# Attention's q, k, v projection turned: tokens on partitions and weights moving, with the attention's stages written in another order

## The chip, the cores and the metric

One core of a Trainium2 chip runs the whole program. The metric is device microseconds for one execution; each kernel's figure is the median of its runs.

## The reference, cut to what matters

A trunk of two layers over x of 512 tokens by 1024 features in float32. The first layer mixes by convolution and pooling, the second by attention; each is followed by a gated MLP of width 2816. The change is in the attention.

```
def rmsnorm(x, g):
    x32 = x.astype(jnp.float32)
    y = x32 * lax.rsqrt(jnp.mean(x32 * x32, axis=-1, keepdims=True) + EPS)
    return (y * g.astype(jnp.float32)).astype(x.dtype)

def dilated_attention(xn, w_qkv, g_q, g_k, w_o, rel_table):
    qkv = (xn @ w_qkv).reshape(B, S, 3, N_HEADS, HEAD_DIM).astype(jnp.float32)
    q = rmsnorm(qkv[:, :, 0], g_q)
    k = rmsnorm(qkv[:, :, 1], g_k)
    v = qkv[:, :, 2]
...
    return o.reshape(B, S, D).astype(xn.dtype) @ w_o
```

There are 16 heads of 64 features. xn is the RMS norm of x over its 1024 features; q and k are normalised again, for each token and head. What is left out above is softmax(q k / 8 + bias) v over three dilated windows, merged.

## The kernel before

Every matrix product is done as three products of fp32r parts: an operand is split into its rounded value (`xh`, `wh`, `bh`) and the rest (`xl`, `wl`, `bl`), and hi x hi + hi x lo + lo x hi is summed in PSUM. `product` (L1082) issues the three: the weight tile of 128 x 128 is stationary, 512 tokens move, so results have features on partitions. Weights arrive by DMA (queue of SP) in four slots `raw0` to `raw3`, one "unit" each; ScalarE rounds a unit into `wh` (`round_unit`, L461, recorded at L466) and GpSimd subtracts to get `wl` (`rest`, L429, at L431). A slot's unit may be rounded when TensorE has used the one before (`s_unit`), and a load waits for GpSimd (`s_lo`).

The attention runs over 8 pairs of heads. Each engine has its instructions written out by hand in a function `stage(p, ...)`; the order in it is the order on the engine, and semaphores join the engines. For a pair the weights are four units: q (1024 columns), k (1024), v in two halves (512 each). TensorE's stage (L1316) does this: q's, k's and v's projections in pieces (`qkv_part`); the column sums of the squares of q and k (L1360: fp32 matmuls with two columns moving, 16 records a pair) into `bank3`; the norm factors, widened by VectorE to 64 columns each, turned onto features by `spread_norm` (L1389, twice 4 transposes); v turned to tokens by `turn_v` (L1380, 4 transposes). Between these stand the heads of the pairs in front: `score_blocks` (L1283, L1284: 8 products of 512, 384, 128 and 256 columns), `transposes` of the probabilities (L1294, 10 of 128 columns), `outputs` (L1312, 8 products into `obank`).

For a head the chain is: scores on TensorE; `scores` on VectorE (L968: adds the bias, takes the maximum, four pieces); `exponentials` on ScalarE (L699); `probabilities` on VectorE (L974 and L976); `transposes` on TensorE; `round_pt` on ScalarE (L716, two pieces) and `rest_pt` on VectorE (L982, two pieces), after which the score bank `spt` is free for the next head (`s_ptl`) and `outputs` can run; then `round_output` on ScalarE (L681) and `rest_output` on VectorE (L1041, L1044), after which the bank `obank` is free for the next head's `outputs` (`s_ol`).

Once a pair, VectorE computes 16 columns of reciprocal roots with small operations (L1005, L746 to L753), widens them (`widen`, L1052), multiplies (`normalise`, L1058), and makes the rests of q, k and v (L1018, L1031, L997).

At the end of the attention the output projection `w_o` begins (`wo_part`): its parts stand between the last heads' steps.

## Time and profile before

| | us |
|---|---|
| median of 3 runs (1132.41 to 2936.12) | 1132.81 |
| profiled execution | 1132.44 |
| its span in the trace | 1130.6 |
| TensorE busy | 1124.8 |
| VectorE busy | 582.0 |
| ScalarE busy | 487.7 |
| GpSimd busy | 461.7 |
| attention, first projection to last output, about | 504 to 742 in the span |

The page lists each engine's busy time, then the span in 40 slices, then groups of instructions by source line. A timeline lists single instructions, with equal neighbours merged (xN) and, in brackets, how long the engine was idle before and what released it. TensorE's records overlap: a matmul's row lasts until its result has drained, so the time that one takes from the engine is the distance to the next start. PE is TensorE, PEld its weight loads, DVE is VectorE, ACT ScalarE, POOL GpSimd.

### The profile page before, as it was taken

The page shows a single profiled execution, that of the slowest core. Times are in us where ns is not written, and L with a number is a line of the kernel's source. Part 1 is how long each engine was busy: PE and PEld are TensorE (multiplying, and loading weights), DVE is VectorE, ACT ScalarE, POOL GpSimd, SP SyncE. Part 2 cuts the span into 40 slices and gives each one's busy share as a digit, 9 for nine tenths or more (in the row PEclk, how much of TensorE's full clock was granted, in tenths as well). Part 3 has the DMA queues.
Part 4 walks back from the last instruction along what each step waited for, and adds up shares of the span by engine and source line. Part 5 has one row for each costly group of instructions (what it writes and reads, how often), then busy time and mean ns, then how long its engine had stood idle before and what let it go on. Part 6 is the DMA issues. An engine that isn't in the chain of part 4 may idle for free.

```text
span 1130.6 us, 16046 instructions
## 1 busy us (share of the span) xinstructions
PE 1124.8 (99%) x5228; PEld 936.7 (83%) x5228; DVE 582.0 (51%) x1047; ACT 487.7 (43%) x750; POOL 461.7 (41%) x221
## 2 busy tenths in 40 slices
PE   9999999999999999999999999999999999999998
PEld 7788888888888888888888888878888888888887
DVE  6875754545445412225777777777844545450000
ACT  5333444444444432324666666644534444341220
POOL 4454534354443445443223332134544344434442
PEclk9999999999999999999999999999999999999999
DMA  8232322322322233332322223122332222223331
GB/s 267 83 106 93 112 77 95 107 93 93 110 78 92 63 108 98 102 109 70 92 75 74 74 88 100 64 75 93 112 111 90 96 95 90 95 63 104 100 100 76
DMA packets 38925, 108.11 MB, mean 96 GB/s; under 512 B 4272, under 2 KB 7344, under 8 KB 38896
## 3 DMA queue, kind: packets, MB, share of 16 engines
q1 hardware_dynamic: 36560, 103.49, 28.7%
q10 hardware_dynamic: 2336, 4.24, 1.3%
q8 instruction: 17, 0.28, 0.1%
q14 instruction: 12, 0.10, 0.0%
HBM read 105.57 MB, written 2.15 MB: 95 GB/s over the span
## 4 chain that ended last, share of the span: by engine, by line
issue 45%; PE 33%; POOL 20%; DMA 1%; POOLq 0%; SPq 0%; ACT 0%; DVE 0%; DVEq 0%
POOL wl L431 20%; PE bank L1087 7%; PE bank L1086 7%; PE bank L1085 7%; PE spt L1085 4%; PE spt L1086 4%; PE spt L1087 4%; DMA raw<-w_in 1%; SPq L361 0%; POOLq L430 0%; POOLq L436 0%; PE obank L1087 0%; PE obank L1086 0%; PE obank L1085 0%; SPq L368 0%
## 5 line engine op out<-in xcount | busy, mean ns | idle before, releaser
L431 POOL TENSOR_TENSOR wl<-raw,wh 128x1024 fp32r<-128x1024 f32 (+2 forms) x214 | 457.5, 2144 | 644.2 <-ACT wh L466 644.2
L1085 PE MATMUL bank<-xh,wh 128*128 128x512 f32 x992 | 390.5, 394 | 0.0
L1087 PE MATMUL bank<-xh,wl 128*128 128x512 f32 x992 | 386.6, 390 | 0.0
L1086 PE MATMUL bank<-xl,wh 128*128 128x512 f32 x992 | 386.2, 389 | 0.0
L466 ACT ACTIVATE wh<-raw 128x1024 fp32r<-128x1024 f32 (+2 forms) x214 | 201.3, 945 | 145.1 <-PE spt L1087 139.4
L1087 PEld LDWEIGHTS bank<-xh,wl 128*128 128x128 f32 x992 | 186.2, 188 | 39.2
L1086 PEld LDWEIGHTS bank<-xl,wh 128*128 128x128 f32 x992 | 186.4, 188 | 37.4
L1085 PEld LDWEIGHTS bank<-xh,wh 128*128 128x128 f32 x992 | 186.3, 188 | 37.2 <-issue 0.4
L908 DVE TENSOR_TENSOR work<-bank,rstd 128x512 f32<-128x512 f32 x88 | 60.6, 691 | 225.0 <-PE bank L1087 223.1
L1085 PE MATMUL spt<-bh,wh 128*128 128x512 f32 x440 | 171.5, 390 | 0.4 <-POOL wl L431 0.3
L1086 PE MATMUL spt<-bl,wh 128*128 128x512 f32 x440 | 171.2, 389 | 0.0
L1087 PE MATMUL spt<-bh,wl 128*128 128x512 f32 x440 | 171.2, 389 | 0.0
L915 DVE SCALAR_TENSOR_TENSOR work<-work,par 128x512 f32<-128x512 f32 x176 | 128.5, 786 | 2.4 <-ACT work L582 1.8
L880 DVE TENSOR_TENSOR x<-spt,x 128x512 f32 (+1 forms) x27 | 18.6, 690 | 207.9 <-PE spt L1087 207.9
L1085 PEld LDWEIGHTS spt<-bh,wh 128*128 128x128 f32 x440 | 82.6, 188 | 18.3 <-POOL wl L431 0.7
L582 ACT ACTIVATE work<-work,par 128x512 f32<-128x512 f32 x44 | 35.9, 816 | 143.0 <-DVE work L908 143.0
L1087 PEld LDWEIGHTS spt<-bh,wl 128*128 128x128 f32 x440 | 82.6, 188 | 17.1
L1086 PEld LDWEIGHTS spt<-bl,wh 128*128 128x128 f32 x440 | 82.6, 188 | 17.1
L578 ACT ACTIVATE work<-work,par 128x512 f32<-128x512 f32 x44 | 35.9, 817 | 55.9 <-DVE work L908 55.9
L588 ACT ACTIVATE work<-work 128x512 f32<-128x512 f32 x44 | 27.9, 634 | 55.4 <-DVE work L915 55.4
L487 ACT ACTIVATE xh<-x,par 128x512 fp32r<-128x512 f32 (+1 forms) x24 | 17.4, 723 | 53.5 <-DVE acc L772 53.3
L772 DVE TENSOR_TENSOR acc<-acc,sq 128x512 f32<-128x512 f32 x24 | 40.0, 1668 | 0.0
(155 smaller groups left out, 938.3 us busy)
## 6 DMA issues: line engine op xcount, KB each, us to landing
raw<-w_up SPq DMA_DIRECT2D x88, 512.0 KB, 3.2
raw<-w_down SPq DMA_DIRECT2D x32, 384.0 KB, 3.1
raw<-w_down SPq DMA_DIRECT2D x32, 320.0 KB, 2.9
raw<-w_qkv SPq DMA_DIRECT2D x16, 512.0 KB, 3.6
raw<-w_in SPq DMA_DIRECT2D x14, 512.0 KB, 4.2
raw<-w_out SPq DMA_DIRECT2D x8, 512.0 KB, 3.2
raw<-w_qkv SPq DMA_DIRECT2D x16, 256.0 KB, 2.8
work<-bias_rows ACTq DMA_DIRECT2D x16, 256.0 KB, 3.1
```

Of the source, the lines that this page charges most:

```text
L431: nc.gpsimd.tensor_tensor(wl[s][:, 0:n], raw[s][:, 0:n], plain(wh[s][:, 0:n]), ALU.subtract).then_inc(s_lo, 1)
L466: nc.scalar.activation(wh[s][:, 0:n], raw[s][:, 0:n], ACT.Copy).then_inc(s_hi, 1)
L578: nc.scalar.activation(ug, zg[j][:, 2:], ACT.Identity, bias=col(i * 16 + (c + 3)), scale=col(i * 16 + (c + 2))).then_inc(s_id, 1)
L582: nc.scalar.activation(uu[j], zu[j][:, 2:], ACT.Identity, bias=col(i * 16 + (c + 7)), scale=col(i * 16 + (c + 6))).then_inc(s_id, 1)
L588: nc.scalar.activation(sg, ug, ACT.Silu).then_inc(s_silu, 1)
L772: nc.vector.tensor_tensor(acc[:], acc[:], squares, ALU.add).then_inc(s_acc, 1)
L880: nc.vector.tensor_tensor(tile(x, n), block_bank, tile(x, n), ALU.add).then_inc(s_x, 1)
L908: nc.vector.tensor_tensor(buf[:, 2:], bank[2 * j + n][:], rstd[:], ALU.mult).then_inc(s_z, 1)
L915: nc.vector.scalar_tensor_tensor(u, z[:, tap:tap + SEQ], col(i * 16 + (c + 4 * n + tap)), u, ALU.mult, ALU.add).then_inc(done, 1)
L1085: mm(dst, wh[s][:, w], hi, start=first, stop=False)
L1086: mm(dst, wh[s][:, w], lo, start=False, stop=False)
L1087: return mm(dst, wl[s][:, w], hi, start=False, stop=last)
```

## The change

The projection is turned. The 128 tokens of a tile of `xh` or `xl` are now stationary, and the pair's weights of q, k and v move together as 3 x 128 columns, so a product has 384 columns and its result has tokens on partitions: `token_product`, L1337 to L1339. There are four token tiles, done two at a time (`tokens`, `tokens_end`). A pair's four units now hold two k each for q, k and v (`QKV` is 768 columns in every slot; a load moves three pieces of 256 columns).

With tokens on partitions, v needs no turn, and the norm is per partition: ScalarE's `evacuate` copies q and k (256 columns), squares them (256) and rounds v scaled by the layer's norm factor (128); VectorE sums the squares (`sums`, two reductions of 512), computes 16 factors (`norm_factors`, twelve small operations), multiplies in place (`normalise`, 512 columns for q and for k), and takes v's rest in four pieces (`rest_v`). TensorE then turns q and k into `bank2` and `bank3` (`turn`, 4 transposes each); ScalarE rounds each half from there (`round_q`, `round_k`, `copy_k`), VectorE takes the rests (`rest_q`, `rest_k`). The sums by matmul, `spread_norm`, `widen`, `turn_v` and one `norm_spread` are gone.

All four engines' stages are written in a new order; loops over pairs are written out.

```diff
-QKV = (SLOT, SLOT, SLOT // 2, SLOT // 2)
+QKV = (6 * P,) * RING
...
+            def evacuate(pair, t):
+
+                b = token_bank(pair, t)
+                token_done(act, pair, t)
+                if pair >= 2:
+                    act.wait_ge(s_qt, pair - 1)
+                    act.wait_ge(s_kt, pair - 1)
+                at = slice(t * 2 * P, (t + 1) * 2 * P)
+                nc.scalar.activation(qk[pair % 2][:, at], bank[b][:, 0:2 * P], ACT.Copy).then_inc(s_qc, 1)
...
+                nc.scalar.activation(qksq[:, at], bank[b][:, 0:2 * P], ACT.Square).then_inc(s_qs, 1)
...
+                nc.scalar.activation(v_heads(pair, t, lo=False), v_part(b), ACT.Copy,
+                                     scale=small[:, 3, t:t + 1]).then_inc(s_vh, 1)
...
+            def stage(p):
+
+                new, mid, old, end = p < PAIRS, 1 <= p <= PAIRS, p >= 2, p >= PAIRS - 1
+                if new:
+                    evacuate(p, 0)
+                    evacuate(p, 1)
+                if mid:
+                    copy_k(p - 1, 0)
+                if old:
+                    round_output(p - 2, 0)
+                if mid:
+                    round_q(p - 1, 0)
+                    round_k(p - 1, 0)
+                if old:
+                    round_pt(2 * (p - 2) + 1)
+                if mid:
+                    round_k(p - 1, 1)
+                if new:
+                    round_weights(p + 1, 0)
+                if p == PAIRS:
+                    keep_w_o()
+                if mid:
+                    round_q(p - 1, 1)
+                if mid and end:
+                    copy_k(p - 1, 1)
+                if new:
+                    round_weights(p + 1, 1)
+                if mid:
+                    exponentials(p - 1, 0)
+                if new:
+                    evacuate(p, 2)
+                    evacuate(p, 3)
+                if mid and not end:
+                    copy_k(p - 1, 1)
+                if old and end:
+                    round_output(p - 2, 1)
+                if new and not end:
+                    round_weights(p + 1, 2)
+                if mid:
+                    round_pt(2 * (p - 1))
+                if new and end:
+                    round_weights(p + 1, 2)
+                if new:
+                    round_weights(p + 1, 3)
+                if old and not end:
+                    round_output(p - 2, 1)
+                if mid:
+                    exponentials(p - 1, 1)
...
+            def stage(p):
+                old = p >= 2
+                if old:
+                    transposes(2 * (p - 2))
+                tokens(p, 0, 0, 3)
+                if old:
+                    score_blocks(p - 2, 1)
+                tokens(p, 0, 3, 6)
+                tokens_end(p, 0)
+                if old:
+                    outputs(p - 2, 0)
+                turn(p - 1, 0)
+                turn(p - 1, 1)
+                tokens(p, 1, 0, 1)
+                if old:
+                    transposes(2 * (p - 2) + 1)
+                tokens(p, 1, 1, 4)
+                score_blocks(p - 1, 0)
+                tokens(p, 1, 4, 6)
+                tokens_end(p, 1)
+                if old:
+                    outputs(p - 2, 1)
...
+            transposes(2 * end - 2)
+            pe.wait_ge(s_vl, TB * PAIRS)
             wo_part(0, 0, 5)
+            wo_part(1, 0, 2)
+            score_blocks(end - 1, 1)
+            turn(end, 0)
+            turn(end, 1)
+            wo_part(1, 2, 5)
+            outputs(end - 1, 0)
             transposes(2 * end - 1)
             wo_part(0, 5, 6)
...
+            wo_part(1, 5, 6)
+            score_blocks(end, 0)
+            outputs(end - 1, 1)
```

The first `stage` above is ScalarE's, the second TensorE's. VectorE's stage, for pair p's new tokens, runs: `rest_v` 0 and 1, `probabilities` of the older pair's second head, `sums`, `rest_q` and `rest_k` of the first half, `rest_pt`, `scores` of p - 1's first head, `rest_output`, `probabilities`, `rest_v` 2, `sums`, `rest_v` 3, `rest_q` and `rest_k` of the second half, `rest_pt`, `rest_output`, `scores` of its second head, `norm_factors`, `normalise`. In the stage of the last pair, `rest_q` and `rest_k` stand ahead of the second `sums`, and `norm_factors` ahead of `rest_pt`.

Three places in the order of the built programs. First TensorE in a full stage, before: the sums of squares stand between v's projection and a head's scores (`par` holds the identity and the columns of 1/64; `work` holds q and k squared).

```order
L1087 MATMUL bank<-xh,wl 128x512
L1354 REGISTER_ALU
L1360 MATMUL bank<-par,work 128x2 [waits s_vl,s_qs]
L1360 MATMUL bank<-par,work 128x2 x7
L1281 ISA [waits s_kh,s_ql]
L1283 MATMUL spt<-bh 128x512 [waits s_ptl]
```

After, in a full stage, the turns of q and k stand between a head's outputs and the next products.

```order
L1440 MATMUL obank<-bl 128x128
L1397 MATMUL bank<-par,work 128x128 [waits s_ql,s_qn]
L1397 MATMUL bank<-par,work 128x128 x3
L1397 MATMUL bank<-par,work 128x128 [waits s_kl,s_kn]
L1397 MATMUL bank<-par,work 128x128 x3
L1337 MATMUL bank<-wh,xh 128x384 [waits s_vl]
L1338 MATMUL bank<-wl,xh 128x384
L1339 MATMUL bank<-wh,xl 128x384
```

The sums are gone, the turns have come, and the products have 384 columns of weights moving.

Second, VectorE at the attention's end, before, from the rests of the transposed probabilities (`spt`) of pair 6's second head to the scores of pair 7's first (`work` is the score tile).

```order
L982 TENSOR_TENSOR bl<-spt,bh 128x512 [waits s_pth]
L982 TENSOR_TENSOR bl<-spt,bh 128x768 [waits s_pth]
L1041 TENSOR_TENSOR sq<-obank,bh 64x512 [waits s_ol,s_oh]
L1044 TENSOR_TENSOR bl<-obank,sq 64x512 [waits s_of]
L965 MEMSET gate 128x1 [waits s_s,s_ta]
L968 ISA work,nmax<-spt,work 128x512
```

The same place after.

```order
L1023 TENSOR_TENSOR bl<-spt,bh 128x768 [waits s_pth]
L1050 SCALAR_TENSOR_TENSOR bh<-bank,gqs,bh 64x512 [waits s_qh]
L1057 SCALAR_TENSOR_TENSOR bl<-bank,par,bh 64x512 [waits s_kd,s_kh]
L1005 MEMSET gate 128x1 [waits s_s,s_ta]
L1008 ISA work,nmax<-spt,work 128x512
L1008 ISA nmax 128x1
L1008 ISA work,nmax<-spt,work 128x384
L1008 ISA nmax 128x1
L1008 ISA work,nmax<-spt,work 128x128
L1008 ISA nmax 128x1
L1008 ISA work,nmax<-spt,work 128x256
L1008 ISA nmax 128x1
```

The rest of the output (`obank`), which stood ahead of the scores, now comes after them, and `rest_q` and `rest_k` stand ahead.

Third, TensorE at that place after: the end of pair 7's first scores, then the outputs of pair 6's second head.

```order
L1411 MATMUL spt<-bh 128x256
L1412 MATMUL spt<-bl,bh 128x256
L1440 MATMUL obank<-bh,bl 128x512 [waits s_ptl,s_ol]
L1440 MATMUL obank<-bl 128x512
L1440 MATMUL obank<-bh,bl 128x384 [waits s_ptl]
```

As before, nothing stands between the two; the wait `s_ol` is for VectorE's rest of the output of pair 6's first head.

## Rows read from the trace of the kernel before

**Rows 1.** The page: busy time of each engine, and the granted TensorE clock by slice.
```profile
PE 1124.8 (99%) x5228; PEld 936.7 (83%) x5228; DVE 582.0 (51%) x1047; ACT 487.7 (43%) x750; POOL 461.7 (41%) x221
PEclk9999999999999999999999999999999999999999
```

**Rows 2.** Timeline of TensorE, one pair: start us, us, engine line op out<-in xcount.
```profile
622.75 1.84 PE L1360 MATMUL bank<-par,work 128*128 128x2 f32 x16
624.46 0.49 PE L1283 MATMUL spt<-bh 128*128 128x512 f32 x1
...
627.82 0.60 PE L1389 MATMUL bank<-par,work 128*128 128x128 f32 x4
628.17 0.47 PE L1085 MATMUL bank<-xh,wh 128*128 128x512 f32 x1
628.49 0.39 PE L1086 MATMUL bank<-xl,wh 128*128 128x512 f32 x1
...
649.64 1.84 PE L1360 MATMUL bank<-par,work 128*128 128x2 f32 x16
```

**Rows 3.** Timeline of TensorE, score products of 512 and 384 columns in succession.
```profile
639.62 0.39 PE L1284 MATMUL spt<-bl,bh 128*128 128x512 f32 x1
639.85 0.33 PE L1283 MATMUL spt<-bh 128*128 128x384 f32 x1
640.02 0.34 PE L1284 MATMUL spt<-bl,bh 128*128 128x384 f32 x1
```

**Rows 4.** The page's costliest groups: weight loads of the projections (busy, mean ns).
```profile
L1087 PEld LDWEIGHTS bank<-xh,wl 128*128 128x128 f32 x992 | 186.2, 188 | 39.2
```

**Rows 5.** Timeline of TensorE near the attention's end.
```profile
740.18 0.40 PE L1312 MATMUL obank<-bl 128*128 128x512 f32 x1
740.75 0.44 PE L1312 MATMUL obank<-bh,bl 128*128 128x384 f32 x1 [0.17 <-DVE bl L982]
```

**Rows 6.** Timelines of VectorE and (last but one) ScalarE, one pair.
```profile
624.63 0.17 DVE L1005 TENSOR_TENSOR small<-bank,epsv 128x16 f32<-128x16 f32 x1 [0.67 <-PE bank L1360]
...
626.93 1.29 DVE L1052 SCALAR_TENSOR_TENSOR work<-small 128x512 f32<-128x512 f32 x2
...
629.17 0.69 DVE L968 CUSTOM_DVE_ANT_0 work<-spt,work 128x512 f32<-128x512 f32 x1
...
630.81 0.69 DVE L1058 TENSOR_TENSOR work<-bank,work 128x512 f32<-128x512 f32 x1
...
632.96 0.18 DVE L974 RECIPROCAL rden<-den 128x4 f32<-128x4 f32 x1
...
634.37 0.68 DVE L1028 TENSOR_TENSOR work<-bank,rstd 128x512 f32<-128x512 f32 x1
...
636.16 1.30 ACT L716 ACTIVATE bh<-spt 128x512 fp32r<-128x512 f32 x2 [0.80 <-PE spt L1294]
...
636.79 1.66 DVE L982 TENSOR_TENSOR bl<-spt,bh 128x512 fp32r<-128x512 f32 x2 [0.43 <-ACT bh L716]
```

**Rows 7.** Groups by shape: ScalarE's roundings from PSUM, GpSimd's rests (busy, mean ns).
```profile
L716 ACT ACTIVATE bh<-spt 128x768 fp32r<-128x768 f32 x12 | 9.8, 820 | 0.0
L716 ACT ACTIVATE bh<-spt 128x512 fp32r<-128x512 f32 x12 | 7.2, 603 | 4.2 <-PE spt L1294 4.0
...
L431 POOL TENSOR_TENSOR wl<-raw,wh 128x768 fp32r<-128x768 f32 x32 | 58.8, 1841 | 73.1 <-ACT wh L466 73.1
```

**Rows 8.** Timelines of VectorE and (last) GpSimd behind the attention.
```profile
761.06 0.68 DVE L772 TENSOR_TENSOR acc<-acc,sq 128x512 f32<-128x512 f32 x1
761.66 0.68 DVE L880 TENSOR_TENSOR x<-spt,x 128x512 f32<-128x512 f32 x1
762.60 2.26 DVE L766 SCALAR_TENSOR_TENSOR xl<-x,par,xh 128x512 fp32r<-128x512 f32 x1 [0.25 <-ACT xh L487]
764.78 2.88 DVE L772 TENSOR_TENSOR acc<-acc,sq 128x512 f32<-128x512 f32 x1
...
761.90 5.21 POOL L431 TENSOR_TENSOR wl<-raw,wh 128x1024 fp32r<-128x1024 f32 x2 [3.52 <-ACT wh L466]
```

More of the change, by code:

```diff
@@ L565, in ffn @@
             def ffn(layer, up, down):
-                keep = 2 * layer + 1
+                keep = layer + 2
                 def hidden(i, j, first=False):
@@ new lines, in turn @@
+            def turn(pair, which):
+                if which:
+                    pe.wait_ge(s_kn, pair + 1)
+                    pe.wait_ge(s_kl, 2 * pair)
+                else:
+                    pe.wait_ge(s_qn, pair + 1)
+                    pe.wait_ge(s_ql, 2 * pair)
+                if pair == 0:
+                    pe.wait_ge(s_vl, TB)
+                for t in range(TB):
+                    at = t * 2 * P + which * P
+                    last = nc.tensor.transpose((qbank, kbank)[which][:, t * P:(t + 1) * P],
+                                               qk[pair % 2][:, at:at + P], ident)
+                last.then_inc((s_qt, s_kt)[which], 1)
@@ L1399, in wo_part @@
+            first_tokens()
+            for p in range(1, PAIRS):
+                stage(p)
             def wo_part(n, k0, k1):
```

517 lines of the change are left out of this document (235 added, 282 removed).

## The prediction

> **What bounds the kernel now.** I read the page first. TensorE's matmuls are busy 1124.8 of 1130.6 us and the granted clock stands at its full level (9) in all 40 slices, while VectorE, ScalarE and GpSimd are at 51, 43 and 41% [rows 1]. Nothing that shortens another engine's work can help unless TensorE waits for it. Then the timeline of TensorE in the attention. Matmuls overlap, so what one costs is the distance between starts, not its "busy" time: 512 columns cost 0.23 us (0.227 over long stretches), 384 columns 0.17, although each brings its own weight load [rows 3]. A pair of heads takes 649.64 - 622.75 = 26.89 us, without a wait [rows 2]. So the sum is TensorE's work removed and added, plus every wait that the new order opens.
>
> **The products.** Before: 3 outputs x 8 k x 3 products of 512 columns, 72 x 0.227 = 16.3 us a pair. After: 4 token tiles x 8 x 3 of 384 columns, 96 x 0.170 = 16.3 us. I take 0, from the 384-column row, which is of this size with the same kind of load; its moving operand lies in one piece, though, and here it is three pieces of 128. Below there is no gain, as both rows stand at 0.44 ns a column. Above is the 0.188 of a weight load [rows 4], if loads stopped hiding behind the shorter products: 0.018 x 768 = +13.8 us.
>
> The Trainium skill ("TensorE: Matmul & The Clock Gate", Back-to-back issue gap) gives a warm gap of N/2.4 + 2.5 ns, a fixed cost for each matmul that speaks against 96 small ones. It would add 24 x 2.5 ns = 60 ns a pair, 0.5 us in all; the rows show 227 and 170 ns, proportional to columns. The sum goes by the rows.
>
> **Removed from TensorE, a pair.** The column sums of squares (L1360): 624.46 - 622.75 = 1.71, and the matmul after such a block starts 0.09 late (628.49 - 628.17 = 0.32 against 0.23): 1.80. Two spreads of the norm factor (L1389): 628.17 - 627.82 = 0.35, with the 0.09 is 0.44 each: 0.88. The turn of v, four transposes of the same form: 0.44. Together 3.12, eight times: 25.0. One spread of the layer's norm: 0.4. **Added:** turns of q and k, eight transposes: 0.35 + 4 x 0.11 + 0.09 = 0.88, eight times 7.0. **Net -18.4.** Before also has six starts of TensorE that come 0.25 to 0.45 late at the attention's two ends (one of them: 740.75 - 740.18 = 0.57 where 0.23 is due [rows 5]), 1.8 together, at places that are gone: with them -20.2. No wait at all would make the span 1110.4.
>
> **Waits in a full stage.** The new period is 26.89 - 2.23 = 24.66. VectorE loses two widened factors, v's scaling and v's rest (four 0.69 ops) and gains two reductions and four v rests of 0.28: about the same load. Two chains decide. (1) Last transpose of P to the next scores: ScalarE starts 0.3 after it, then two roundings and two rests, 636.16 to 638.45, 2.3 us [rows 6]; 18 products cover 3.07. ScalarE is up to 0.5 late here. Slack about 0.4. (2) Scores to `turn`: biased scores 629.17 to 630.81 (1.64), twelve small ops of 0.21 (2.5; before's eleven run 624.63 to 626.93), two normalising ops 1.3, starting 0.3 after the last matmul: 5.8; 30 products and the outputs (5.1 + 1.23) cover 6.3. Slack 0.4 to 0.5. I take 0 for both. If the unseen forms (evacuations, 128-column rests at 0.28, a reduction at 0.6) cost 0.5 more per stage, six stages lose about 1 to 3 us.
>
> **Waits at the head.** ScalarE now takes two evacuations before it rounds the next pair's first weights (0.82), then comes GpSimd's rest (1.84) [rows 7]. ScalarE needs 0.603 for 512 columns and 0.820 for 768, so about 0.39 for 256 and 0.28 for 128: an evacuation of 256 + 256 + 128 is 1.1. So 0.2 + 2.2 + 0.8 + 1.9 = 5.1 us after the first tile is done, and TensorE has 18 products = 3.06 left: waits 2.1. GpSimd then runs four rests back to back, into VectorE's twelve small ops. What that costs stands in [rows 8]: during GpSimd's two ops, 5.21 us together, VectorE's ops with two SBUF inputs took 2.26 and 2.88, where the latter (L772) takes 0.68 alone, and one passed at each end of a GpSimd op. So the first `turn` is some 1.0 late. Stage 2 has no previous outputs (1.23 us of cover) and loses about 0.9. Head: 4.0.
>
> "GPSIMD Engine Reference" (Key points) of the Trainium skill says GpSimd shares its SBUF interfaces with VectorE, with contention for VectorE instructions that have two SBUF inputs. By that rule, the trace agrees: L880, which reads one input from PSUM and runs into the same GpSimd op, keeps its 0.68.
>
> **Waits at the tail**, where W_o's parts replace the products. Time T runs from the transposes of pair 6's first head. (a) TensorE is free at 1.1 but waits for VectorE's last v rest. VectorE ends the probabilities at -0.25 (1.41 us, [rows 6]), then has one v rest, q's and k's rests (1.4), a reduction and the v rest: 2.45. Wait 1.35. (b) The twelve small ops come next. ScalarE ends `round_pt` at 2.6 and W_o's unit 2 (1.05) at 3.7; GpSimd takes units 2 and 3 from 3.7 to 8.5. Seven small ops pass, one more at 6.1, the others after 8.5: 9.2. `rest_pt` 1.66 comes behind: scores, due at 7.2, start at 9.9 and stop for the second half: 3.1, and `turn` 0.3 for k. (c) Next scores: only 6 products (1.36) cover the chain of 2.3, and ScalarE has a copy, an output and q, k (0.6 each) in front: 1.5. (d) `outputs` of head 13 stands right behind those scores and waits for `rest_output` of head 12, which VectorE now has after `rest_q`, `rest_k`, `scores`. From the last matmul: 0.3 + 1.7 + 1.4 (two 0.69 ops) = 3.4 at least, and 1.1 more as the rests in front wait for ScalarE's copies: 4.5. Before, the same `rest_output` stood ahead of the scores. (e) The last `outputs` waits for `rest_output` behind `rest_pt`: 0.3 + 2.3 + 1.4 less 1.36 of cover: 2.5. Tail: 13.2. Bounds: nothing for (b) if the engines miss each other, so 9.8; with 0.5 more on each, 16.
>
> **Sum.** -20.2 + 4.0 + 13.2 = -3.0: span 1127.6. The profiled execution took 1132.44 outside its span of 1130.6, the median is 1132.81; so +2.2: **1130 us**.
>
> DMA: the same bytes, in 1 KB pieces; a slot has about 20 us for a transfer that lands in under 4, so it costs nothing, and would cost only if landing took five times as long.
>
> **Rivals.**
> *A, most waits are covered.* If (b) misses and ScalarE and VectorE run earlier than I stacked them, (d) and (e) keep 3.4 + 2.5 and the head 2: 7.9 to 10 us instead of 17.2: 1120 to 1123; the floor with none is 1112.6. For it: before's own order has only 1.8 us of such waits. Against: (d) and (e) follow from the order alone.
> *B, slower than before.* The moving operand in three pieces costs x more per product. At x = 4 ns (3 us over 768) the gain is gone; at 18 ns, a weight load that no longer hides, it is 1144; at 33 ns it passes 2%. For it: no row has a moving operand in pieces. Against: 384 columns with loads run at 0.17. The same side is reached by 0.5 us a stage and a half more in both chains.
> *C, it does not keep GpSimd and VectorE apart.* Counted from a full stage's start, ScalarE ends its roundings at 3.7 and 19.6, so GpSimd (1.84 later) at 5.5, before the small ops at 7.4, and at 21.4 to 21.8, before the probabilities at 22.4. If the latter meet, a stage loses up to 2, six of them 12: 1142.
>
> **How the numbers follow.** Forecast (1124 to 1133) 0.50; A (1112 to 1124) 0.28; B and C, within 2% (1133 to 1155) 0.17; beyond 2% slower 0.02; more than 2% faster 0.03, for which even a stage without waits is not enough (1112.6 against 1110.2) unless products cost under 0.167. 2% is about what a measurement of this kernel can tell from no change. Faster 0.03, within 2% 0.95, slower 0.02. The range leaves out the low part of A and the high part of B and C: 1117 to 1137.
>
> **What would show it.** The stage period on TensorE at 24.7; 384-column starts 0.170 apart; L1360 and L1389 gone and no gap in stages 3 to 6; gaps of 2 us at the first tokens of pair 1, and at the tail 1.4, 3, 1.5, 4.5, 2.5 before the named calls, the fourth ended by VectorE's rest of the output. VectorE ops of over 1 us would show a meeting with GpSimd. A period over 25.2 or starts over 0.175 apart would prove the sum wrong, as would a gap under 3 us at (d).

## The result, and the profile after

The changed kernel takes 1134.13 us (median of 16 runs, 1132.59 to 1137.03), the kernel before 1132.41 (16 runs): ratio 1.002, 95% interval 1.0013 to 1.0027. It is slower by 0.2%, where the forecast was faster by 0.2%. The time lies inside the range of 1117 to 1137 us, but 1.1 us above the band that the forecast itself was given (1124 to 1133), in the one that had been given to rivals B and C.

| | before, us | after, us |
|---|---|---|
| median | 1132.41 | 1134.13 |
| profiled execution | 1132.44 | 1133.13 |
| its span | 1130.6 | 1131.0 |
| TensorE busy | 1124.8 | 1112.0 |
| one pair in the full stages | 26.89 | 24.83 |
| waits of TensorE at the attention's two ends (between starts, less what is due), about | 1.8 | 16 |

The page of the changed kernel: busy time, and the granted TensorE clock in 40 slices, beside [rows 1].

```profile
PE 1112.0 (98%) x5256; PEld 947.1 (84%) x5256; DVE 589.9 (52%) x1071; ACT 498.0 (44%) x805; POOL 461.8 (41%) x221
PEclk9999999999999999999999999899999999999999
```

TensorE is busy for 12.8 us less and the span is 0.4 longer. One of the clock's digits is an 8; before, all were 9.

The timeline of TensorE of the changed kernel, one pair (start us, us, engine line op out<-in xcount), which answers to [rows 2]: the first and the last of 30 products of 384 columns, then the turn of this pair and of the next.

```profile
622.73 0.34 PE L1337 MATMUL bank<-wh,xh 128*128 128x384 f32 x1
...
627.76 0.33 PE L1339 MATMUL bank<-wh,xl 128*128 128x384 f32 x1
...
629.16 0.51 PE L1397 MATMUL bank<-par,work 128*128 128x128 f32 x3
...
654.00 1.06 PE L1397 MATMUL bank<-par,work 128*128 128x128 f32 x8
```

29 distances between starts take 627.76 - 622.73 = 5.03 us, 0.1734 each. The period is 654.00 - 629.16 = 24.83 us after rounding, the same for each of the five periods from 554.66 to 678.83, with no listed wait in them.

The waits of TensorE from 500 to 760 us in the changed kernel (engine line waited for: us in total, times, longest).

```profile
PE obank L1440 <- DVE bl L1077: 6.7, 2, 4.4
PE spt L1411 <- DVE bl L1023: 3.5, 2, 2.5
PE bank L1153 <- DVE bl L1064: 1.7, 1, 1.7
PE bank L1337 <- POOL wl L448: 1.5, 1, 1.5
PE spt L1153 <- POOL wl L448: 0.3, 1, 0.3
```

The fourth is the head: pair 1's first tokens wait for GpSimd's rest. The first three are the tail, called (a) to (e) as in the prediction: (a) is L1153, (b) and (c) L1411, (d) and (e) L1440. The last was there before. The list counts an engine's idle time, 13.7 us in all; between starts, where a matmul's overlap with the next is lost too, the waits come to 16.

Last, the windows of the tail of the changed kernel (us, busy time of TensorE, its loads, VectorE, ScalarE, GpSimd, then the granted clock, DMA share, GB/s).

```profile
640.00:700.00 60.00, 58.04 (x357) 55.72 (x355) 51.48 (x137) 44.62 (x100) 20.53 (x10) 1.00 0.33 102
700.00:710.00 10.00, 7.68 (x36) 6.63 (x37) 8.51 (x27) 3.11 (x10) 0.07 (x1) 0.83 0.28 99
710.00:716.00 6.00, 4.12 (x23) 2.90 (x21) 4.15 (x6) 5.34 (x10) 0.00 (x0) 0.99 0.00 0
716.00:720.00 4.00, 0.45 (x1) 0.45 (x2) 3.85 (x14) 2.29 (x8) 0.00 (x0) 0.50 0.00 0
720.00:724.00 4.00, 4.00 (x16) 3.45 (x16) 2.13 (x6) 0.59 (x1) 0.00 (x0) 0.66 0.00 0
724.00:760.00 36.00, 33.40 (x163) 27.63 (x162) 22.05 (x35) 13.70 (x25) 10.00 (x4) 1.00 0.15 46
```

The clock is at its lower level, 1.2 of 2.4 GHz, in two stretches: the trace's clock record has them from 702.24 to 705.65 and from 715.89 to 722.72 us. Products of 512 columns started 0.427 us apart there instead of 0.227. The prediction had no term for this.

The other executions have no such record of places, but each has its mean granted clock, and the time goes with it: the changed kernel's run at 0.997 took 1132.59 us, eight of the nine at 0.995 (the profiled one too) 1133.1 to 1134.2, and the two at 0.992 took 1136.17 and 1137.03. The median is 1.0 us above the profiled execution, so by the medians the kernels are 1.7 us apart and by the profiled executions 0.7.

### The profile page after: what moved, and what is told of

The parts are those of the page before. It is cut to its first block, busy times and chain, and to the rows that moved or that the text cites. A ratio compares the mean times of both kernels' runs of the same rounds, so it can differ in the third digit from the quotient of the medians.

```text
span 1131.0 us, 15745 instructions
## 1 busy us (share of the span) xinstructions
PE 1112.0 (98%) x5256; PEld 947.1 (84%) x5256; DVE 589.9 (52%) x1071; ACT 498.0 (44%) x805; POOL 461.8 (41%) x221
## 4 chain that ended last, share of the span: by engine, by line
issue 46%; PE 33%; POOL 19%; DMA 1%; POOLq 0%; SPq 0%; ACT 0%; DVE 0%; DVEq 0%
POOL wl L448 19%; PE bank L1153 7%; PE bank L1154 7%; PE bank L1155 7%; PE spt L1153 4%; PE spt L1155 4%; PE spt L1154 4%; DMA raw<-w_in 1%; SPq L377 0%; POOLq L447 0%; POOLq L453 0%; PE obank L1154 0%; PE obank L1153 0%; PE obank L1155 0%; SPq L384 0%
## 5 line engine op out<-in xcount | busy, mean ns | idle before, releaser
L1153 PE MATMUL bank<-xh,wh 128*128 128x512 f32 x800 | 311.7, 390 | 0.0
L1155 PE MATMUL bank<-xh,wl 128*128 128x512 f32 x800 | 311.3, 389 | 0.0
L1154 PE MATMUL bank<-xl,wh 128*128 128x512 f32 x800 | 311.2, 389 | 0.0
L1153 PEld LDWEIGHTS bank<-xh,wh 128*128 128x128 f32 x800 | 150.2, 188 | 31.7 <-issue 0.4
L1155 PEld LDWEIGHTS bank<-xh,wl 128*128 128x128 f32 x800 | 150.2, 188 | 31.4
L1154 PEld LDWEIGHTS bank<-xl,wh 128*128 128x128 f32 x800 | 150.2, 188 | 30.7
L1153 PE MATMUL spt<-bh,wh 128*128 128x512 f32 x440 | 171.5, 390 | 0.4 <-POOL wl L448 0.3
L1153 PEld LDWEIGHTS spt<-bh,wh 128*128 128x128 f32 x440 | 82.6, 188 | 18.2 <-POOL wl L448 0.7
L1337 PE MATMUL bank<-wh,xh 128*128 128x384 f32 x256 | 87.7, 342 | 1.7 <-POOL wl L448 1.5
L1339 PE MATMUL bank<-wh,xl 128*128 128x384 f32 x256 | 85.7, 335 | 0.0
L1338 PE MATMUL bank<-wl,xh 128*128 128x384 f32 x256 | 85.7, 335 | 0.0
```

What stands on the lines that cost most here:

```text
L1153: mm(dst, wh[s][:, w], hi, start=first, stop=False)
L1154: mm(dst, wh[s][:, w], lo, start=False, stop=False)
L1155: return mm(dst, wl[s][:, w], hi, start=False, stop=last)
L1337: mm(dst, xh[:, k, rows], pair_weights(wh, k), start=k == 0, stop=False)
L1338: mm(dst, xh[:, k, rows], pair_weights(wl, k), start=False, stop=False)
L1339: return mm(dst, xl[:, k, rows], pair_weights(wh, k), start=False, stop=k == KT - 1)
```

## The experiments

All ratios are to the kernel before, whose median beside these runs was 1132.4 to 1132.8 us. The changed kernel stands at 1134.1 by its 16 runs, and "saved" and "cost" below are against that. Spans and rows are of the profiled execution.

### One VectorE step ahead, for wait (d)

```diff
                 if p == PAIRS:
+                    rest_output(p - 2, 0)
                     rest_q(p - 1, 1)
                     rest_k(p - 1, 1)
                 if mid:
                     scores(p - 1, 0)
-                if old:
+                if old and p < PAIRS:
                     rest_output(p - 2, 0)
```

(For p > PAIRS the call stands right ahead of `rest_output(p - 2, 1)`, where it stood.)

> The changed kernel with one move on VectorE at the attention's end: the rest of the output of pair 6's first head stands ahead of the q and k rests and the scores of pair 7. In the trace of the changed kernel TensorE waits 4.66 us (714.90 to 719.55) at the outputs behind it, and the clock was at half (0.50 and 0.66 of full in the rows from 716 to 724). Theory 1 (the order alone makes the wait, and the long idle stretch costs clock on top): the wait falls to about 0.5, the next transposes wait 0.5 to 1, the second low stretch of the clock goes (about 1.5 us); together 3 to 5 us faster than the changed kernel, so 0.997 to 0.999 of the kernel before (the changed one is 1.002). Rival (ScalarE's and VectorE's chain bounds the whole end, so a wait removed comes back at the next step): under 1 us faster, ratio 1.001 or more.

Measured: 1129.52 us, ratio 0.9973 (0.9963 to 0.9984), 4.6 us saved. In the changed kernel the wait reads so: TensorE's last score product, its next instruction, and VectorE's step that it waited for.

```profile
714.90 0.28 PE L1412 MATMUL spt<-bl,bh 128*128 128x256 f32 x1
719.55 0.79 PE L1440 MATMUL obank<-bh,bl 128*128 128x512 f32 x1 [4.38 <-DVE bl L1077]
```

```profile
718.80 0.69 DVE L1077 TENSOR_TENSOR bl<-obank,sq 64x512 fp32r<-64x512 f32 x1
```

The same place with the step ahead, and the transposes of head 14 behind it:

```profile
715.50 0.28 PE L1415 MATMUL spt<-bl,bh 128*128 128x256 f32 x1
716.03 0.50 PE L1443 MATMUL obank<-bh,bl 128*128 128x512 f32 x1 [0.25 <-DVE bl L1077]
...
721.51 0.76 PE L1425 MATMUL spt<-par,work 128*128 128x128 f32 x5 [0.51 <-DVE work L1017]
```

4.65 us between starts became 0.53, and 0.7 came back at the next transposes. Wait (d) is one by order: VectorE had the work ready to do and stood in `rest_q`, `rest_k` and `scores`. The gain is in the expected range. The clock did only half of what was expected: the long stretch behind (d) went, but one of 3.4 us (737.70 to 741.11) now came behind wait (e).

### The moving operand in one piece (rival B)

The load puts the same bytes contiguously, so that the product's 384 columns are one piece instead of 3 x 128. The host lays the weights out to match, and the products are the same.

```diff
-                pair = w_qkv[bass.ds(i, 1)].rearrange("a p (w n) -> (a p) w n", w=3)
                 for s in range(RING):
-                    load(U_QKV + i * 4 + s, s, raw[s][:, 0:6 * P].rearrange("p (w n) -> p w n", w=3),
-                         pair[:, :, 2 * s * P:(2 * s + 2) * P])
+                    load(U_QKV + i * 4 + s, s, raw[s][:, 0:6 * P],
+                         pick(w_qkv[:, :, 6 * s * P:6 * (s + 1) * P], i))
...
```

(`token_product` takes and writes the 384 columns in a row.)

> The changed kernel with the weights of a pair laid out so that the 384 moving columns lie in one piece instead of three pieces of 128 (host layout, load and views; same products). In the changed kernel the starts of these products lie 0.1735 us apart, where 0.170 was forecast. Theory 1 (the pieces cost): starts 0.170 to 0.171 apart, full stage 24.83 to about 24.5, 768 x 0.003 = 2.5 us faster, ratio near 1.000. Rival (it is the short product behind a weight load, whatever the layout): starts 0.1735 apart, no change, ratio 1.002.

Measured: 1133.91 us, ratio 1.0022 (1.0012 to 1.0031): the same as with three pieces. TensorE's products with one piece, in their timeline:

```profile
630.97 0.33 PE L1338 MATMUL bank<-wh,xl 128*128 128x384 f32 x1
631.14 0.33 PE L1336 MATMUL bank<-wh,xh 128*128 128x384 f32 x1
631.31 0.33 PE L1337 MATMUL bank<-wl,xh 128*128 128x384 f32 x1
631.49 0.34 PE L1338 MATMUL bank<-wh,xl 128*128 128x384 f32 x1
```

0.52 us for three, 0.173 each, as in the changed kernel. The layout costs nothing; 0.173 is what 384 columns take.

### GpSimd out of the way of the last small operations (wait (b))

```diff
-            rests(U_WO, U_DOWN1, FULL)
+            rest(U_WO, 0)
+            rest(U_WO + 1, 1)
+            rest(U_WO + 2, 2, P)
+            rest(U_WO + 3, 3, P)
+            rests(U_WO + RING, U_DOWN1, FULL)
```

The kernel leaves out 896 of the 1024 columns of `wl` in W_o's units 2 and 3, which keep old values.

> The changed kernel with GpSimd's rests of units 2 and 3 of the output projection cut to 128 of 1024 columns (the other 896 columns of wl keep old values: that part of the computation is left out). In the changed kernel two of VectorE's small operations took 2.38 and 2.31 us beside GpSimd's two rests (4.75 us), and TensorE waited from 699.37 for the next scores. Theory 1 (meeting of GpSimd and VectorE at their SBUF interfaces): the small operations all take under 0.4, the wait of 2.86 before the scores goes, and the low stretch of the clock at 702 to 706 with it; 3 to 5 us faster, ratio 0.997 to 0.999. Rival (VectorE is late for another reason, its q and k rests standing in front): small operations short, but the scores still wait 2 us or more.

Measured: 1132.1 us, ratio 0.9994 (0.9985 to 1.0003), 2.0 us saved, less than the 3 to 5 expected. The changed kernel's timelines of VectorE and of GpSimd at that place:

```profile
695.16 0.18 DVE L789 TENSOR_TENSOR small<-guess 128x16 f32<-128x16 f32 x1
695.37 2.38 DVE L790 TENSOR_TENSOR small<-small 128x16 f32<-128x16 f32 x1
697.79 2.31 DVE L792 SCALAR_TENSOR_TENSOR small<-small,guess 128x16 f32<-128x16 f32 x1
700.14 0.17 DVE L789 TENSOR_TENSOR small<-small 128x16 f32<-128x16 f32 x1
```

```profile
695.32 4.75 POOL L448 TENSOR_TENSOR wl<-raw,wh 128x1024 fp32r<-128x1024 f32 x2 [4.98 <-ACT wh L483]
```

Two operations on 16 columns, due in 0.17 us, each last until one of GpSimd's (2.4) ends. With GpSimd's rests cut to 0.46 and 0.50 us the same two took 0.44 and 0.17 and one later 0.32, and the scores followed the products without a wait:

```profile
700.11 0.39 PE L1159 MATMUL bank<-bh,wl 128*128 128x512 f32 x1
700.34 0.39 PE L1415 MATMUL spt<-bh 128*128 128x512 f32 x1
```

So the first theory held for the wait. Of its 2.6 us, 0.4 came back at the outputs of head 12, and the low stretch at 702 went, but another (737.93 to 741.35) came behind wait (e).

### The last output's rest ahead (wait (e))

```diff
+                if p > PAIRS:
+                    rest_output(p - 2, 0)
                 if old:
                     rest_pt(2 * (p - 2) + 1)
...
-                if old:
+                if old and p <= PAIRS:
                     rest_output(p - 2, 0)
```

> The changed kernel with the rest of the output of pair 7's first head moved ahead of the last rests of the transposed probabilities on VectorE. The changed kernel waits 2.71 us (from 737.88) before the last outputs. Theory 1: the wait falls to about 1.0, as the rests of the probabilities alone take 2.3 us behind the transposes and 1.4 are covered; 1.5 to 2 us faster, ratio about 1.0005. Rival (the time comes back in the wait for GpSimd at 749.93): the later wait grows by what this one gives, ratio 1.002.

Measured: 1132.88 us, ratio 0.9999 (0.999 to 1.0008), 1.25 us saved, where 1.5 to 2 were expected. The outputs at (e) in the changed kernel, then here:

```profile
740.59 0.50 PE L1440 MATMUL obank<-bh,bl 128*128 128x512 f32 x1 [2.31 <-DVE bl L1077]
```

```profile
740.01 0.47 PE L1442 MATMUL obank<-bh,bl 128*128 128x512 f32 x1 [0.78 <-DVE bl L1023]
```

The distance between starts at (e) fell from 2.71 to 1.17, with 0.2 more behind it, and what ends the wait is now VectorE's rest of the probabilities (L1023).

### The three together

The edits of the first, third and fourth runs at once.

> The three single edits to the last pairs at once: output rest of head 12 ahead of the q and k rests, GpSimd's rests of W_o's units 2 and 3 cut to 128 columns (the rest of W_o's low parts in these units is left out), and the last output rest ahead of the last pt rest. Theory 1 (each removes a wait of its own): the gains add, 4.6 + 2.0 + 1.25 = 7.9 us off 1134.1, 1126 us, ratio 0.994 to 0.995. Theory 2 (one chain decides): the sum is under 6 us and a wait appears at the transposes of head 14, or after, of what is missing.

Measured: 1123.75 us, ratio 0.9924 (0.9909 to 0.994): 10.4 us saved, more than the 7.9 that the three saved apart and that theory 1 had expected here. Its trace has the clock full up to TensorE's last products, where each single edit left two low stretches. The 2.5 above their sum is put down to the clock; that is argued from the trace, not isolated. That made the clock the next question.

### One wait filled with work

The 16 products have no use: they add a wrong term to one part of the W_o product.

```diff
             score_blocks(end, 0)
+            for n in range(16):
+                mm(bank[1][:], wh[1][:, 0:P], bh[:, MIX, :], start=False, stop=False)
             outputs(end - 1, 1)
```

> 16 more products of 512 columns (3.6 us at 0.227 us each) between the last score blocks of head 14 and the outputs of head 13, where TensorE otherwise waits 4.4 us for VectorE's rest of the output of head 12; they add a wrong term to one part of the W_o product, and change no wait. Theory 1 (the granted clock falls because TensorE has stood idle, 714.9 to 719.55 us): the outputs start as before at 719.5, the stretch of half clock from 716 to 722.7 us is gone (its outputs 0.16 us apart again), and the time is 1.5 us shorter although 3.6 us of work is added, ratio to the kernel before 1.000 instead of 1.0015; the spread of its runs is also narrower than the changed kernel's 4.4 us. Theory 2 (the dip comes from something else, such as the chip's load as a whole): the same dip, or one elsewhere, and 1134 us.

Measured: 1134.01 us, ratio 1.0012 (1.0003 to 1.0021). TensorE's timeline with wait (d) filled:

```profile
715.26 3.82 PE L1495 MATMUL bank<-bh,wh 128*128 128x512 f32 x16
719.82 0.50 PE L1440 MATMUL obank<-bh,bl 128*128 128x512 f32 x1 [0.74 <-DVE bl L1077]
720.15 0.39 PE L1440 MATMUL obank<-bl 128*128 128x512 f32 x1
```

At that place the first theory held: the outputs start where they did, and run at the full clock (the first 0.50, where it took 0.79). The time did not fall, since now a low stretch from 739.70 to 743.11 followed wait (e), which had none in the changed kernel's profile. The expectation of 1.5 us less was wrong, and left both theories standing; the spread shrank from 4.4 to 2.1 us.

### Three waits filled

The same, with wrong terms in three parts of the W_o product: 11 such products ahead of `score_blocks(end - 1, 1)`, 18 ahead of `outputs(end - 1, 1)` and 10 ahead of `wo_part(3, 6, 7)`.

> Products of 512 columns with no use put into the three longest waits of the tail: 11 before the scores of head 13 (2.5 us), 18 before the outputs of head 13 (4.1 us), 10 before the last outputs (2.3 us); they add wrong terms to three parts of the W_o product and release nothing earlier. Theory 1 (the granted clock falls on TensorE's long waits, and each of the three can bring a dip): no stretch at half clock from 700 to 745 us, the ends of the waits stay where they are, and the time is 1131 us (1130.5 to 1131.5), 3 us less than the changed kernel although 8.9 us of work is added, with a spread under 1.5 us. Theory 2 (the dip is only moved, to whatever comes next, as from 716 to 740 us when one wait was filled): a dip of 3.4 us or more remains somewhere before 760 us, and the time is 1132.5 to 1134 us.

Measured: 1131.07 us (1130.53 to 1131.61), ratio 0.9986 (0.9977 to 0.9995): 3.1 us less than the changed kernel with 8.9 us of useless work added, and a spread of 1.1 us instead of 4.4. The windows of this kernel, columns as above:

```profile
700.00:710.00 10.00, 9.42 (x54) 7.54 (x53) 8.39 (x26) 4.10 (x12) 0.00 (x0) 1.00 0.29 93
710.00:724.00 14.00, 12.67 (x61) 9.84 (x60) 10.38 (x24) 7.23 (x18) 0.00 (x0) 1.00 0.00 1
724.00:745.00 21.00, 20.95 (x108) 17.59 (x107) 10.85 (x25) 7.46 (x16) 2.40 (x1) 1.00 0.08 25
```

All 11 runs have a mean granted clock of 0.999 or 1.000. So in this kernel the clock falls because of TensorE's waits, and its fall is worth 3.1 us by the medians, apart from the waits themselves. By the spans of the profiled executions (1128.5 against 1131.0) it is 2.5: without the low stretch at 702 the outputs of head 12 wait 0.4 longer.

### GpSimd made to meet the small operations

```diff
-            rests(U_QKV, U_WO, QKV)
+            nc.gpsimd.memset(waste[:], 0.0).then_inc(s_waste, 1)
+            with pool.Fori(0, PAIRS) as i:
+                for s in range(RING):
+                    rest(i * RING + (U_QKV + s), s, QKV[s])
+                for n in range(4):
+                    pool.wait_ge(s_waste, i * 4 + (n + 1))
+                    nc.gpsimd.tensor_tensor(waste[:], par[:, 0:384], par[:, 0:384],
+                                            ALU.subtract).then_inc(s_waste, 1)
```

> After each pair's fourth rest GpSimd does four more useless subtractions of 384 columns (0.95 us each by 1.84 us for 768), so that it works up to 626.5 us in the stage shown and meets VectorE's small operations, which there run from 624.75 to 627.2; all results stay the same. Theory 1 (work apart is worth something: two-input operations of GpSimd and VectorE hold each other up, as the two small operations of 2.38 and 2.31 us in the last pair showed): one or two of the 0.17 us operations take 0.9 us each or more, the normalised values come about 1.5 us late, 0.6 of it is slack before the turn, and each of the six full stages is 0.6 to 1.2 us longer: the period 25.4 to 26.0 us instead of 24.83, 4 to 8 us in all, 1138 to 1142 us, ratio 1.005 to 1.009. Theory 2 (such a meeting costs VectorE next to nothing in a full stage): period 24.83 and 1134 us.

Measured: 1139.57 us, ratio 1.0061 (1.0045 to 1.0076), 5.4 us lost. In a full stage of this kernel, GpSimd's four and two of VectorE's small operations:

```profile
627.97 3.59 POOL L479 TENSOR_TENSOR waste<-par 128x384 f32<-128x384 f32 x4
```

```profile
630.12 0.53 DVE L1046 SCALAR_TENSOR_TENSOR small<-small,epsv 128x16 f32<-128x16 f32 x1
630.69 0.18 DVE L794 TENSOR_SCALAR guess<-small 128x16 int32<-128x16 int32 x1
630.90 0.68 DVE L795 TENSOR_SCALAR small<-small 128x16 f32<-128x16 f32 x1
```

A full stage is 25.15 to 25.37 us, 0.3 to 0.5 more, less than the 0.6 to 1.2 expected. The profiled execution's span is 6.6 longer than the changed kernel's: 2.1 in the turn of pair 1, which now waits for the small operations, 1.7 in a low stretch of the clock right behind it (535.11 to 538.52), 1.9 in five full stages, and 0.9 in smaller ones. The direction is theory 1's; two of the three larger terms are not those that it wrote down, so that the time lay in its range is partly luck.

### The same four elsewhere

The four subtractions between GpSimd's second and third rest of each pair.

> The same four useless subtractions of 384 columns for each pair as in the run in which they met the small operations, now between GpSimd's second and third rest, where its queue is idle for 4.4 us (639.2 to 643.5 in the stage that follows) and VectorE reads PSUM or works with one tensor operand; all results stay the same. Theory 1 (it is the meeting that costs, not GpSimd's work as such): the small operations run in 2.5 us again, the period is 24.83 us or up to 0.1 more, the turn of pair 1 waits 0.4 us instead of 2.5, 1134 to 1135.5 us, ratio 1.001 to 1.003. Theory 2 (any added GpSimd work costs, as more traffic or through a later third rest): 1138 us or more, as when it met the small operations.

Measured: 1144.93 us, ratio 1.0107 (1.0092 to 1.0123), 10.8 us lost. It was meant as the harmless place, and neither theory holds as written. The small operations run in 0.17 again, but the four met another group, VectorE's scaling of the probabilities. That group in the changed kernel, then here, then GpSimd here:

```profile
615.41 1.28 DVE L1017 TENSOR_SCALAR work<-work,rden 128x512 f32<-128x512 f32 x4
```

```profile
647.76 2.87 DVE L1028 TENSOR_SCALAR work<-work,rden 128x512 f32<-128x512 f32 x4
```

```profile
646.65 3.63 POOL L479 TENSOR_TENSOR waste<-par 128x384 f32<-128x384 f32 x4
```

An operation with one tensor from SBUF and a scalar column is held just as one with two tensors. The transposes start late by what the slack does not cover, and a full stage takes 25.90 us, 1.07 more: 6.5 in all up to the tail. At the head the third rest stands behind the four, which makes a distance of 3.0 between two products where 0.2 is due. One more low stretch of the clock (750.55 to 753.97) adds some 1.7. That is 11.0, of 11.6 more in the span of the profiled execution.

### Two only, beside operations that read PSUM

As in the run that met the small operations, with `range(2)`.

> Two useless subtractions of 384 columns (0.9 us each) for each pair, right behind GpSimd's fourth rest: in the full stage from 622.6 to 624.4 us, beside VectorE's maxima over the scores (which read PSUM) and ahead of its small operations at 624.75; all results stay the same. Theory 1 (a meeting costs where VectorE's operation has all its tensor operands in SBUF, whether one or two, and nothing where one is in PSUM, as the last two runs' rows read): period 24.83 in the full stages, and only in pair 1 the small operations are held some 0.5 to 1.5 us longer; 1134 to 1136 us, ratio 1.001 to 1.003. Theory 2 (added GpSimd work costs about 0.27 us for each of its operations in a stage, wherever it lies: 1.07 us for four): period 25.2 to 25.4, 1137 us or more.

Measured: 1136.55 us, ratio 1.0034 (1.002 to 1.0048), 2.4 us more than the changed kernel's median, but with an interval that overlaps its own (1.0013 to 1.0027). In the full stages it is the first theory: period 24.83, and VectorE's maxima, which read `spt` in PSUM, keep their 0.69 beside GpSimd:

```profile
623.76 1.74 POOL L479 TENSOR_TENSOR waste<-par 128x384 f32<-128x384 f32 x2
```

```profile
624.29 0.69 DVE L1017 CUSTOM_DVE_ANT_0 work<-spt,work 128x512 f32<-128x512 f32 x1
...
626.14 0.17 DVE L794 TENSOR_SCALAR guess<-small 128x16 int32<-128x16 int32 x1
```

In the profiled execution the turn of pair 1 comes 1.1 later and there is a third low stretch (742.44 to 745.85), worth up to 1.7. The time lay 0.5 over the expected range; the one run with a mean granted clock of 0.997 instead of 0.994 or 0.995 took 1133.98.

### A new order for the two ends

Nothing is left out here. In pair 0 ScalarE rounds pair 1's first three units ahead of the evacuations. At the end VectorE computes the factors and normalises pair 7 ahead of pair 6's q and k rests; ScalarE rounds W_o's units 2 and 3 once that is done, so GpSimd starts on them later; and TensorE has products or turns between a score block and what needs its result. The core of it, ScalarE's, VectorE's and TensorE's parts in turn (the calls that the new ones replace further down are left out):

```diff
+                if p == 0:
+                    for s in range(3):
+                        round_weights(1, s)
                 if new:
                     evacuate(p, 0)
                     evacuate(p, 1)
...
                 if new and end:
+                    act.wait_ge(s_qn, PAIRS)
+                    act.wait_ge(s_kn, PAIRS)
                     round_weights(p + 1, 2)
...
+                if p == PAIRS:
+                    probabilities(p - 2, 1)
+                    rest_q(p - 1, 1)
+                    rest_pt(2 * (p - 2) + 1)
+                    rest_output(p - 2, 0)
+                    scores(p - 1, 0)
+                    rest_k(p - 1, 1)
+                    probabilities(p - 1, 0)
+                    rest_output(p - 2, 1)
+                    rest_pt(2 * (p - 1))
+                    scores(p - 1, 1)
+                    return
...
                 if p == PAIRS - 1:
                     norm_factors()
+                    normalise(p, 0)
+                    normalise(p, 1)
-                if mid and not end:
+                if mid:
                     rest_q(p - 1, 1)
                     rest_k(p - 1, 1)
...
             wo_part(0, 0, 5)
-            wo_part(1, 0, 2)
-            score_blocks(end - 1, 1)
+            wo_part(1, 0, 3)
             turn(end, 0)
             turn(end, 1)
-            wo_part(1, 2, 5)
+            score_blocks(end - 1, 1)
+            wo_part(1, 3, 5)
             outputs(end - 1, 0)
-            transposes(2 * end - 1)
             wo_part(0, 5, 6)
             wo_part(1, 5, 6)
+            transposes(2 * end - 1)
+            pe.wait_ge(s_ql, 2 * PAIRS)
+            wo_part(2, 0, 4)
             score_blocks(end, 0)
             outputs(end - 1, 1)
...
```

> The last pairs put in a new order on all three engines, nothing left out: the statistics and normalising of pair 7 run ahead of the q and k rests of pair 6 on VectorE, the finished head outputs go out ahead of q/k rests and scores, GpSimd gets units 2 and 3 of W_o only when VectorE has normalised, and TensorE has W_o products or the two turns between each score block and what needs its result; in pair 0 the rounding of pair 1's first three units goes ahead of the evacuations. Theory 1 (the changed kernel's tail waits, 13.2 us in all, are waits by order, and with them go the two stretches of half clock, 3.2 us): with the order laid out on paper the tail needs about 37 us from the transposes of head 12 to the end of attention instead of 50; 10 to 15 us go, a time of 1119 to 1124 us, ratio to the kernel before 0.988 to 0.993, and the clock full from 700 to 740 us. Theory 2 (the tail is bound by the chain probabilities, transposes, copies, outputs, rests, whatever the order): about 5 us as the two single reorderings together gave, 1128 to 1129 us, and the waits turn up at other places with the same sum.

Measured: **1118.91 us** (1118.87 to 1121.31), ratio 0.9886 (0.9871 to 0.9901), 15.2 us less than the changed kernel and 13.5 less than the kernel before. The waits of TensorE in it from 500 to 760 us, and the clock in 40 slices:

```profile
PE obank L1477 <- DVE bl L1050: 1.6, 1, 1.6
PE spt L1459 <- DVE work L1044: 0.4, 1, 0.4
PE spt L1190 <- POOL wl L448: 0.3, 1, 0.3
PE bank L1190 <- DVE bh L1077: 0.3, 1, 0.3
```

```profile
PEclk9999999999999999999999999999999999999999
```

13.7 us of listed waits became 2.6, and the clock stays full here (one of its four runs, at a mean granted clock of 0.998, took 1121.31). The period is 24.83 as in the changed kernel, so all of the gain is at the two ends. The theory that a chain binds the tail whatever the order falls; what each move of this order is worth by itself is not shown. The largest wait left, 1.6, is that of the outputs of the last head, behind VectorE's rest of its probabilities.

## Why the prediction was wrong

The sum, term by term, in the profiled execution:

| term | forecast, us | measured, us |
|---|---|---|
| removed and added work, late starts of before | -20.2 | -20.8 (what is left over) |
| products of 384 columns for those of 512 | 0 | +2.4 |
| waits in full stages | 0 | 0 |
| head | +4.0 | +2.3 |
| tail | +13.2 | +13.2 |
| clock at the lower level | none | +3.3 |
| span against before | -3.0 | +0.4 |

The time was forecast to fall and rose. Two steps of the sum failed: the price of the products, put at 0, and the price of the waits, which left out the clock. Errors the other way, in the head and in what is left over, hid 2.3 us of these 5.7.

**The products, mis-sized by 2.4.** The forecast took 0.170 us from [rows 3], one distance between two starts that are printed to 0.01 us. With the measured 0.1734 a pair's products take 96 x 0.1734 = 16.65 us beside 72 x 0.227 = 16.34: 0.30 more, 2.4 in eight pairs. The number was to be had: 62 such starts in the trace of before have a median distance of 0.175. It went on to the step "proportional to columns": 384 columns cost 0.1734 - 0.75 x 0.227 = 0.003 more than their share of 512, so the line through both has a fixed part of four times that, 12 to 13 ns a matmul; the starts of products of 256 columns, 0.120 apart by their median, lie on it. Its cause was not tested beyond the layout, which is excluded. The Trainium skill ("TensorE: Matmul & The Clock Gate", Back-to-back issue gap) has a fixed part in its form for an isolated gap, N/2.4 + 2.5 ns, which the prediction set aside; the runs agree that there is one, and show it larger.

**The clock, missing.** This is the larger step that failed: "TensorE's work removed and added, plus every wait that the new order opens" prices each wait at its own length. The low stretches cost half of the time in which TensorE works in them: 3.41/2 = 1.7, and (722.72 - 719.55)/2 = 1.6, 3.3 together; with the waits filled 3.1 came back by the medians. Before, the clock was full in all slices of the profiled execution [rows 1], so no row had the price, and nothing asked what longer waits would do. The clock is not always full there either: 12 of 67 runs of the kernel before that stand beside the experiments have a mean granted clock of 0.998, and take about 0.9 us more than the others. The Trainium skill ("TensorE: Matmul & The Clock Gate", HAM oscillation) describes a kernel whose waits bring the clock down again; the trace agrees, with 0.50 from 716 to 720 us in a kernel that is 98% busy.

**The head, 1.7 too much.** The first tokens of pair 1 waited 1.7 (2.1 forecast), the first turn 0.2 (1.0) and stage 2 0.3 (0.9), with 0.1 in a slow first product. The meeting with GpSimd took place: in a timeline of VectorE two small operations lasted 1.75 and 1.76 us.

```profile
524.71 1.75 DVE L785 TENSOR_SCALAR guess<-small 128x16 int32<-128x16 int32 x1
526.50 1.76 DVE L786 TENSOR_SCALAR small<-small 128x16 f32<-128x16 f32 x1
```

TensorE had cover for nearly all of it.

**What is left over.** This term was not measured by itself. A full stage bears on it: 26.89 - 24.83 = 2.06, and with the 0.30 of the products 2.36 us of other work are gone, where 2.23 were forecast; that is 1.0 in eight. Against it, the last of before's late starts (0.45, W_o behind GpSimd) was counted among places that are gone, and is still there.

**The tail, right to the place.** Forecast 1.35, 3.1 + 0.3, 1.5, 4.5, 2.5; measured between starts, less what is due there: 1.9, 2.6, 1.4, 4.5, 2.5 and 0.3 in smaller ones. (a) came 0.5 longer and (b) 0.8 shorter, so that the total agrees so well is partly luck. The places are not: the runs show (b), (d) and (e) each ended by the step that the prediction named. (a) and (c) were not tested one by one.

**The full stages, right.** Period 24.83 for 24.66; the products' price (0.30) explains more than the difference. **Rival A** was wrong for this kernel, as the waits did not close up; the new order shows what it would have been worth. **Rival B** was wrong in its mechanism, as the layout costs nothing, though the time fell in its band, and its way of counting, x more for each product, is where 2.4 us came from. **Rival C** did not come true in the full stages: GpSimd ends at 622.62 and the small operations begin at 624.75, 2.1 later (1.9 forecast). The runs that closed this gap or used the other one lost 0.3 to 1.07 us a stage, so keeping the two apart is worth that much, against meetings of this size.

**The sign.** It hung on -20.2 against 17.2 of waits: a net of 3 between terms of 20, with two unpriced effects of 2.4 and 3.3. A net like that can only be given as "within 2%"; its sign was not known. None of the signs of a wrong sum that the prediction had named appeared (a period over 25.2, starts over 0.175 apart, under 3 us at (d)): none of them looked at the clock.

## What to carry to other kernels

When a wait is opened on the engine that bounds the kernel, price it twice, once at its length and once for what the clock does behind it: here 3.3 us for 13.2 of waits at the tail. Take the price of many equal instructions from a long run of them, since 0.0034 us in a rounded difference is 2.6 us over 768. And when a steady state is shortened by moving work, look at the first and last stages as orders of their own: here they held 15 us, more than the 13.5 by which the best version beats the kernel before.

## What the runs showed of the hardware

- The granted clock fell to its lower level behind some waits of TensorE of 2.5 to 4.7 us between starts, in a kernel that is busy before and after; not behind each of them (3.0 us at 527 us in one run left it full), nor at the same ones in every kernel. In the profiled executions of four kernels, before among them, whose largest distances from 500 to 760 us are 2.0 us or less, it stayed full there. That this holds in every execution is not so: the kernel before has a mean of 0.998 in 12 of 67 runs, and no trace shows where it fell in them.
- The time of an execution goes with its mean granted clock: in the run with GpSimd's rests cut, 1129.32 and 1129.56 us at 0.997, and 1131.75 to 1132.88 in the nine at 0.995 and 0.994. The changed kernel's 16 runs spread over 4.4 us at 0.992 to 0.997, the 11 with three waits filled, at 0.999 or 1.000, over 1.1.
- A VectorE operation that starts beside one of GpSimd's and has its tensors in SBUF lasts about until GpSimd's ends, also a very small one: 16 columns took 2.38, 2.31, 1.76 and 0.68 us beside subtractions of 1024, 1024, 768 and 384 columns, and 0.17 alone. It is so for tensor by scalar too (four took 2.87 us instead of 1.28), but not for operations that read PSUM (0.69 beside GpSimd and alone). The Trainium skill ("GPSIMD Engine Reference", Key points) names two SBUF inputs or a two-port mode as the condition; the prediction used only the first half, which covers neither these four nor the two of 1.75 and 1.76 us at the head, each with one tensor from SBUF. No run here tells in which mode they worked.
- 384 columns cost TensorE 0.173 us, with the moving operand in one piece or in three.
